# The expert layer as two dense products over whole tables instead of gathered rows

## What is computed

```python
def _peer(h, w_q, keys1, keys2, u_tab, v_tab):        # per block of tb = 128 tokens
    qh = (hb @ w_q).reshape(tb, 8, 2, 128)
    s1 = jnp.einsum('thd,nd->thn', qh[:, :, 0], keys1)
    s2 = jnp.einsum('thd,nd->thn', qh[:, :, 1], keys2)
    v1, i1 = lax.top_k(s1, 16)
    v2, i2 = lax.top_k(s2, 16)
    cand = (v1[..., :, None] + v2[..., None, :]).reshape(tb, 8, 256)
    cidx = (i1[..., :, None] * 128 + i2[..., None, :]).reshape(tb, 8, 256)
    best, pos = lax.top_k(cand, 16)
    eidx = jnp.take_along_axis(cidx, pos, axis=-1)
    gates = jax.nn.softmax(best.astype(jnp.float32), axis=-1).astype(hb.dtype)
    act = jax.nn.gelu(jnp.einsum('td,thkd->thk', hb, u_tab[eidx]), approximate=False)
    return jnp.einsum('thk,thkd->td', gates * act, v_tab[eidx])
```

## Time and profile before

| | |
|---|---|
| median of 3 runs | 3188.63 us (3188.34 to 3195.54) |
| span of the profiled execution | 3191.6 us |
| mean granted TensorE clock in it | 0.987 of full speed |
| last query product before the experts ends | 2524.2 us |
| last product with v rows ends | 3180.8 us |
| PE busy in the span | 3008.7 us (94%) |
| DVE, ACT, POOL busy | 1624.6, 814.9, 349.4 us |
| moved by DMA | 584.86 MB |

### The profile page before, as it was taken

How to read it: one execution, slowest core, us unless ns; L and a number is a source line. 1 busy time by engine, 2 the same in 40 slices (tenths; PEclk the granted TensorE clock), 3 DMA queues, 4 the chain that set the end, 5 groups by cost and what they waited for, 6 DMA issues and landing times. The chain is left out here.

```text
span 3191.6 us, 33886 instructions
## 1 busy us (share of the span) xinstructions
PE 3008.7 (94%) x12694; PEld 2114.5 (66%) x12694; DVE 1624.6 (51%) x3601; ACT 814.9 (26%) x1889; POOL 349.4 (11%) x391
## 2 busy tenths in 40 slices
PE   7999999999999999998999999999989999888776
PEld 3666556758888888485876678888877744443222
DVE  3233444367773676413234457543036577677774
ACT  2222244311002100012113430010023354444443
POOL 0000000010000000100000000000000244344442
PEclk9999999999999999999999999999998999999999
DMA  6212111153441544642322134577432799999997
GB/s 240 86 60 66 53 53 53 53 165 119 132 135 57 161 154 131 204 142 89 104 79 80 60 109 158 186 285 277 143 113 95 271 420 420 383 421 420 420 420 311
DMA packets 280769, 584.86 MB, mean 183 GB/s; under 512 B 11736, under 2 KB 231768, under 8 KB 244256
## 3 DMA queue, kind: packets, MB, share of 16 engines
q0 software_dynamic: 51504, 338.98, 27.0%
q1 hardware_dynamic: 229104, 243.73, 23.7%
HBM read 581.58 MB, written 1.08 MB: 183 GB/s over the span
## 5 line engine op out<-in xcount | busy, mean ns | idle before, releaser
L815 PE MATMUL banks<-normed,weight_ring 128*128 128x512 f32 (+1 forms) x1280 | 483.9, 533 | 14.4 <-PEq L322 13.9
L815 PEld LDWEIGHTS banks<-normed,weight_ring 128*128 128x128 f32 x1280 | 242.5, 191 | 233.9 <-issue 223.0
L824 PE MATMUL banks<-weight_ring,normed 128*128 128x256 f32 x1408 | 320.5, 383 | 0.0
L3581 PE MATMUL banks<-weight_ring,work 128*128 128x512 f32 x512 | 248.9, 610 | 56.8 <-ACT work L3450 55.8
L824 PEld LDWEIGHTS banks<-weight_ring,normed 128*128 128x128 f32 x1408 | 265.0, 191 | 54.0 <-issue 19.4
L3581 PE MATMUL banks<-work 128*128 128x512 f32 x512 | 253.3, 617 | 49.9 <-ACT work L3450 48.8
L436 DVE CUSTOM_DVE_ANT_0 work<-work 128x1024 f32<-128x1024 f32 x176 | 209.5, 1224 | 111.4 <-DMA work<-ada_turned 92.6
L2155 PE MATMUL banks<-normed,weight_ring 128*128 128x256 f32 x1088 | 241.0, 385 | 9.9 <-ACT normed L2325 3.8
L2155 PEld LDWEIGHTS banks<-normed,weight_ring 128*128 128x128 f32 x1088 | 209.9, 193 | 40.5 <-issue 6.6
L1660 PE MATMUL banks<-branches,weight_ring 128*128 128x256 f32 (+1 forms) x656 | 210.3, 483 | 3.4 <-PEq L322 3.4
L3581 PEld LDWEIGHTS banks<-weight_ring,work 128*128 128x128 f32 x512 | 87.7, 189 | 167.5 <-ACT work L3450 104.8
(11 more groups left out here) (515 smaller groups left out, 3947.4 us busy)
## 6 DMA issues: line engine op xcount, KB each, us to landing
weight_ring<-w_in SPq DMA_DIRECT2D x98, 1024.0 KB, 5.2
weight_ring<-w_ffn_in SPq DMA_DIRECT2D x44, 1024.0 KB, 5.4
work<-ada_turned POOLq DMA_DIRECT2D x80, 512.0 KB, 3.8
work<-ada_turned POOLq DMA_DIRECT2D x16, 1536.0 KB, 9.6
weight_ring<-w_ffn_out SPq DMA_DIRECT2D x20, 1024.0 KB, 5.2
weight_ring<-w_out SPq DMA_DIRECT2D x12, 1024.0 KB, 5.3
weight_ring<-w_br_ml SPq DMA_DIRECT2D x8, 1024.0 KB, 5.3
weight_ring<-w_br_da SPq DMA_DIRECT2D x8, 1024.0 KB, 5.2
```

What stands on the lines that cost most here:

```text
L815: last = pe.matmul(proj_bank(tile)[:, since:T], w[:, kk, half * P:(half + 1) * P], c.h[:, kk, since:T], start=kk == 0, stop=kk == KT - 1)
L824: last = pe.matmul(proj_bank(tile)[:, x * CHUNK:(x + 1) * CHUNK], c.h[:, kk, j * P:(j + 1) * P], w[:, kk, :], start=kk == 0, stop=kk == KT ...
L3581: last = pe.matmul(c.banks[2 * t + half][:], diag[:, r, :], vrows[r][:, half * 512:(half + 1) * 512], start=e == t * H * K, stop=e == (t + ...
```

## The change

The expert layer no longer fetches the rows of chosen experts. It streams both tables once, whole, through `weight_ring`, in 64 pieces of 1 MB each (`expert_u`, `expert_v`; a piece is called a pair, since it holds 2 x 128 experts). The host lays the tables out for that.

- Products with u: for every pair, `pair_product` computes all 256 experts of the pair for all 256 tokens (16 products of 128x256), and ScalarE's `lift` takes the gelu into `dense`, a sheet of 128 x (128 x 256) fp32 that holds one number for every expert and token. All arrays that it overlays are now parts of one tensor `room`.
- Gates: a token's gates form a 128 x 128 sheet (first index by second index). It is made as a product of two matrices over the token's 128 chosen places: `right`, one-hot in the second index (POOL), and `left`, one-hot in the first index times the gate (VectorE). This is `choose`, one product of 128x128 for each token, 4 tokens to a group. VectorE multiplies `dense` with the group's sheets (`apply_group`), and ScalarE and VectorE place and apply them for the pairs whose gelu comes later (`place_group`, `apply_pair`). The 64 groups are spread over pairs 36 to 63: two groups behind a pair, and three behind 8 of the 28 pairs.
- Products with v: `value_product`, for each of 64 pairs, 2 rows of experts, 2 token tiles and 2 halves one product of 128x512, 512 in all. The last two pairs are ordered by token tile.
- All 16 queries and scores are done before the products with u. The searches run two units at a time, and the numbers of the experts are worked out for 8 heads at once (`name`). POOL issues no DMA in this layer any more.

Core of the diff:

```diff
-        for e in range(2 * H * K):
-            if e % K == 0:
-                pool.wait_ge(c.ranked, e // K + 1)
-            if e >= R:
-                pool.wait_ge(c.expert_done, e - R + 1)
...
-            pool.indirect_dma_start(
-                out=fetched[e % R], out_offset=None, in_=a["experts"],
-                in_offset=bass.IndirectOffsetOnAxis(ap=experts_u[:, e:e + 1], axis=0)
-            ).then_inc(c.gathered[e % R], 16)
+        for group in range(GROUPS):
...
+            if group >= 2:
+                pool.wait_ge(c.chosen, group - 1)
+            for i in range(PEER_GROUP):
+                token = PEER_GROUP * group + i
+                last = pool.tensor_scalar(right[token % (2 * PEER_GROUP)], c.constant("iota"), turned[:, 1, token:token + 1], None,
+                                          ALU.is_equal)
+            last.then_inc(c.right_made, 1)
...
+        def make_left(group):
...
+            if group >= 2:
+                dve.wait_ge(c.chosen, group - 1)
+            for i in range(PEER_GROUP):
+                token = PEER_GROUP * group + i
+                last = dve.tensor_scalar(left[token % (2 * PEER_GROUP)], c.constant("iota"), turned[:, 0, token:token + 1],
+                                         turned[:, 2, token:token + 1], ALU.is_equal, ALU.mult)
+            last.then_inc(c.left_made, 1)
+
+        def apply_group(group):
...
+            dve.wait_ge(c.chosen, group + 1)
+            dve.wait_ge(c.lifted, pairs)
+            part = dense[:, 0:2 * pairs, group_tokens(group)]
...
+        for pair in range(PEER_FIRST, PAIRS):
+            for group in groups_at(pair):
+                if group + 1 < GROUPS:
+                    make_left(group + 1)
+                apply_group(group)
+            apply_pair(pair)
...
+        def pair_product(pair):
+
+            w = weights(16 + pair)
+            if pair >= 2:
+                pe.wait_ge(c.lifted, pair - 1)
+            for i in range(2):
+                for k in range(KT):
+                    last = pe.matmul(c.banks[pair % 2][:, i * NLAT:(i + 1) * NLAT], w[:, k, i * P:(i + 1) * P], hs[:, k, :],
+                                     start=k == 0, stop=k == KT - 1)
+            last.then_inc(c.pair_product, 1)
...
+        def choose(group):
...
+            pe.wait_ge(c.left_made, group + 1)
+            pe.wait_ge(c.right_made, group + 1)
+            if group >= 4:
+                pe.wait_ge(c.chosen_applied, group - 3)
+                pe.wait_ge(c.chosen_placed, group - 3)
+            for i in range(PEER_GROUP):
+                r = (PEER_GROUP * group + i) % (2 * PEER_GROUP)
+                last = pe.matmul(out[:, :, i], right[r], left[r], start=True, stop=True)
+            last.then_inc(c.chosen, 1)
+
+        def value_product(pair, i, t):
+
+            w = weights(16 + PAIRS + pair).rearrange("p k n -> p (k n)")
+            for half in range(2):
+                at = i * D + half * 512
+                last = pe.matmul(c.banks[2 * t + half][:], dense[:, 2 * pair + i, tokens_of(t)], w[:, at:at + 512],
+                                 start=pair == 0 and i == 0, stop=pair == PAIRS - 1 and i == 1)
+            return last
...
+        for n in range(2 * PAIRS):
+            if n >= SLOTS:
+                if n - SLOTS < PAIRS:
+                    sp.wait_ge(c.pair_product, n - SLOTS + 1)
+                else:
+                    sp.wait_ge(c.pair_valued, n - SLOTS - PAIRS + 1)
+            its = c.ring[:, n % SLOTS]
+            if n < PAIRS:
+                sp.dma_start(its, a["expert_u"][n]).then_inc(c.loaded[n % SLOTS], 16)
```

More of the change, by code:

```diff
@@ new lines, in ending @@
+        def ending(t):
+            done = Chain(dve, c.finished)
+            done.n = 6 * t
+            dve.wait_ge(c.expert_done, t + 1)
+            dve.wait_ge(c.row_copied, 8)
+            for half in range(2):
+                part = slice(half * 512, (half + 1) * 512)
+                done.mark(dve.tensor_tensor(acc[:, part], c.banks[2 * t + half][:], gate_row[:, part], ALU.mult))
+            done.wait()
+            done(dve.tensor_tensor(xt[:, t, :], xt[:, t, :], acc, ALU.add))
+            dve.wait_ge(c.finish_rooted, 2 * t + 1)
+            done(dve.tensor_scalar(mean, mean, 1.0 / D, EPS, ALU.mult, ALU.add))
+            done(dve.reciprocal(inverse, mean))
+            dve.wait_ge(c.finish_rooted, 2 * t + 2)
+            done(dve.scalar_tensor_tensor(tokens[:, t, :], xt[:, t, :], mean, gain_row, ALU.mult, ALU.mult))
@@ L3365, in vector @@
         inverted(0)
-        for k in range(KT):
-            out_scale(0, k)
-        search = Search(dve, 0)
-        for _ in search.halves():
-            pass
-        assert search.n == IN_HALVES
-        for _ in chain(search.numbers(), search.weights(1)):
-            pass
-        dve.wait_ge(c.token_copied, 2)
-        for u, t in units:
-            body(u, t)
-        for part in ending(1).values():
-            part()
+        out_scale(0)
+        search([0])
+        for tile in range(KT):
+            added(1, tile)
+        inverted(1)
+        out_scale(1)
+        for first in (1, 3, 5):
+            search([first, first + 1])
+        search([7])
+        name(0)
+        search([8, 9])
+        weigh(0)
+        for first in (10, 12, 14):
+            search([first, first + 1])
+        name(1)
+        weigh(1)
+        make_left(0)
+        for pair in range(PEER_FIRST, PAIRS):
[4 more added lines that the diff above has]
+            apply_pair(pair)
+        for t in range(2):
+            ending(t)
     def scalar(act):
         def copy_query(n):
-            head, first, end = PEER_QUERIES[n]
-            part = slice(first * P, end * P)
+            head, t = QUERIES[n]
             act.wait_ge(c.queried, n + 1)
@@ L3519, in score @@
                 pe.wait_ge(c.score_copied, n - 1)
[L3520 to L3523 removed]
+            for i in range(2):
+                last = pe.matmul(score_bank(n)[:, t, i * P:(i + 1) * P], qh[:, n % 2, i, tokens_of(t)], keys[:, i, :],
+                                 start=True, stop=True)
@@ L3563, in tensor @@
         query(0)
-        turn_tokens(0)
+        out_tile(1, 2, 0, 8)
         score(0)
-        for tile in range(2, KT):
+        for tile in range(3, KT):
             out_tile(1, tile, 0, 8)
@@ new lines, in tensor @@
+        query(3)
+        for tile in range(KT):
+            out_sum(1, tile)
+        score(2)
+        for n in range(4, len(QUERIES)):
+            query(n)
+            score(n - 1)
+        for pair in range(PAIRS):
+            pair_product(pair)
+            if pair == 0:
+                score(len(QUERIES) - 1)
+            if pair in PEER_TURNS:
+                turn_lists(PEER_TURNS.index(pair))
+            for group in groups_at(pair):
+                choose(group)
+        pe.wait_ge(c.chosen_applied, GROUPS)
```

579 lines of the change are left out of this document (273 added, 306 removed).

## The result

The changed kernel takes 3550.8 us in the median (3550.09 to 3558.97), the kernel before, on the same chip, 3190.9. The ratio is 1.113, with a 95% interval of 1.111 to 1.115: 360 us slower, where 3552 us was forecast.

A forecast was written before the change was run, and what follows sets the result against it. Transfers were taken to bound the expert loop (656 us), TensorE close behind at 549.6 busy. Along TensorE's queue, 2523.3 + 55.1 + 446.5 + 58.7 + 15 + 3 + 439.3 + 3.6 + 10.8 = 3555.3, forecast 3552 us, range 3525 to 3640.

The forecast's parts named there:

- 5 between pairs and values: Between the last pair and the first value product: a chain of three short instructions, 3 us.
- Step 2: Products with u on TensorE: 2048 instructions of 128x256 at 0.218 us, 446.5 us, 6.98 us a pair.
- Step 4: In pairs with three groups TensorE stalls for the third group's matrices, 8 times: 10 to 18 us, taken as 15.
- step 6: Products with v on TensorE: 1024 instructions at 0.429 us, 439.3 us, plus 3.6 us for eight turns of rows.
- 3.0 off: Taken from the summed span of 3555.3 us because the runs' median lies 3.0 us under the profiled span: 3552 us.
- my own range: Range of the main case (chance 0.80): 3532 us without stalls and at 0.217, to 3580 with dearer instructions and port rule.
- The port rule: VectorE's two-port instructions and GpSimd's exclude each other, so step 4's stalls would cost 9 us more: 3561 us.
- A cover: VectorE's searches, costed at nothing: ending near 2655 us, ahead of their uses in the pairs by 40 to 100 us.
- A (POOL): POOL bounds pairs 36 to 63 if a one-hot matrix costs 0.91 us or more; 3624 us at 1.25; chance 0.08.
- B (choosing doesn't stream): Each of 512 choosing instructions takes its 0.275 us latency, not 0.112: 83 us more, 3635 us; chance 0.08.
- C (bytes decide): Transfers stay the expert stage's limit and bytes halve, so the kernel gets faster: 2905 us; chance 0.01.
- D: Loads or lists come late so that TensorE isn't the path, adding some tens of us; chance 0.03.

The follow-up runs named there:

- the high halves: Changed kernel, products with u and v reading only the high 16 bits of each fp32 as bf16, one instruction instead of two: 2999.6 us, 0.940 of before.
- the half rows: Kernel before, gathers fetching only the u half of each row, all instructions as before: 3090.2 us, 0.968 of before.

## Why the prediction was right

The forecast of the time and its reason hold: the layer went from a bound by transfers to a bound by TensorE, and the sum along TensorE's queue came out. Its terms, with the working in the prediction, against the changed kernel's rows:

| step | forecast, us | measured, us |
|---|---|---|
| third query ends at | 2523.3 | 2528.8 |
| 1 rest of queries and scores | 55.1 | 54.9 |
| 2 products with u | 446.5 | 442.0 |
| 3 choosing gates, turning lists | 58.7 | 57.8 |
| 4 the eight waits | 15 | 14.9 |
| 5 between pairs and values | 3 | 2.1 |
| 6 products with v, turns of rows | 442.9 | 446.0 |
| 7 the end | 10.8 | 10.1 |
| span | 3555.3 | 3557.2 |

Step 2 is the 960 instructions from 2590.69 to 2797.89, 0.2158 us each, times 2048. The measured rows add up to 3556.6; 0.6 us are left between the steps. Step 4 is eight times the gap from the end of the second group (2866.07 + 16 x 0.1116 = 2867.86) to 2869.72. Step 6 runs from 3101.11 to the last product's end at 3547.1.

**What hit by offset.** The two programs are the same up to the layer, and the changed one got there 5.5 us later in its profile. That is no effect of the change that any run here shows: of the seven variants with the same program up to there, five got there 3 to 6 us earlier than the kernel before, and two 4 us later. The steps themselves were 3.6 us too dear in sum, and the profiled execution lay 6.4 us above the median's time, where I had taken 3.0 off. Plus 5.5, less 3.6, less 3.4: the median's agreement within 1.2 us is partly luck. So is the steps' sum. Step 2 was 4.5 us too dear (0.218 us an instruction, where it took 0.2158) and step 6 was 3.1 us too cheap. And the lower end of my own range, 3532, doesn't follow from its terms: without the stalls (15 us) and at 0.217 us an instruction (2 us) the sum gives 3535.

**Step 6 lacked a term: the clock.** In the first products with v the granted clock was at its lower level:

```profile
3101.00:3107.00 6.00, 5.89 (x8) 2.54 (x9) 0.01 (x1) 0.00 (x0) 0.00 (x0) 0.52 0.00 0
3107.00:3113.00 6.00, 6.00 (x16) 2.65 (x15) 0.00 (x0) 0.00 (x0) 0.00 (x0) 1.00 0.13 29
...
3101.11 23.63 PE L3576 MATMUL banks<-weight_ring,room 128*128 128x512 f32 x48 [1.88 <-issue]
```

TensorE works off half as many instructions in the first 6 us as in the next, and this is the 2.8 us of the first 48: at 0.429 us they would take 20.8. Before the clock fell TensorE had stood still twice within 5 us, the last of the eight waits (1.65 us) and the step from gates to values (1.88). Where the first of these is gone (pairs with two groups only) or 0.93 us long (without POOL's matrices), the same 48 take 20.84 us. In the two variants that keep both (half of the bytes, no VectorE matrices) they take 22.34 and 22.44. So, by these profiles (one of each kernel), the last of the eight waits cost more than its own length.

**Step 4** was right for a half-right reason. The wait is where I put it, and its size too. I had VectorE and POOL both as candidates and POOL between 0.2 and 0.7 us an instruction; it is 0.59 in a row, nearer to my upper end, and POOL alone sets the wait.

**The port rule** was worth 9 us in its own sentence and nothing in the runs.

**A cover was mis-sized.** I let VectorE's searches end near 2655. They ended 30 us later, at 2685:

```profile
2591.35 0.23 DVE L3291 TENSOR_SCALAR normed<-room 128x128 uint32<-128x128 uint32 x1 [19.61 <-ACT room L3395]
...
2641.56 0.29 DVE L3307 TENSOR_REDUCE room<-room 128x8 f32<-128x128 f32 x1 [26.22 <-ACT room L3419]
...
2682.74 2.29 DVE L3301 TENSOR_REDUCE room<-stream 128x128 f32<-128x2048 f32 x1
```

VectorE stands still twice. For 19.6 us it waits in the middle of naming the first token tile's experts, because `name(0)` waits there for the scores of all 16 units. For 26.2 us it waits in `weigh(0)`, which sums the exponentials of the first tile, and these ScalarE makes only when it comes to pair 8. I had read pair 8 as the time by which VectorE must be ready, and overlooked that VectorE's program stops there until ScalarE gets to it. The second wait sets the end: without the first one VectorE would only have come to `weigh(0)` sooner and waited longer. The second half was due at pair 25, at 2583 + 25 x 6.9 = 2756 us, so both cost nothing. With the high halves, where pair 8 comes at about 2600 us and pair 25 at 2643.5, the cover is nearly gone: VectorE has the second tile's sums ready for the exponentials at 2637.7, 6 us ahead, and TensorE waits for no list.

**The rivals.** A (POOL) fell at its condition: 0.60 us an instruction, where it decides from 0.91 on; in the version with cheap products it held. B (choosing doesn't stream) fell: 16 instructions in 1.95 us, 0.112 each, though every fourth column is written. C (bytes decide) fell for this change by the price of TensorE's instructions, as argued, and the high halves show the other side: with those prices cut, the same stream of tables gives 3000 us. The sentence of the Trainium skill (SBUF — State Buffer, "A bandwidth-pool intuition that's wrong"), "HBM is almost always your end-to-end bottleneck", sets HBM against SBUF there and not against TensorE. Read as widely as in rival C, it fits the kernel before (nearly half of TensorE's busy time there gained nothing) and not the one after (half of the tables' bytes gained nothing). D had no place: no wait for a load or a list stands before TensorE's products in the changed kernel.

## What to carry to other kernels

When a stage is bound by one resource, read how far behind it the second one runs before its work is traded: here the gathers held 656 us and TensorE 550 of them, so halving the bytes could give at most the 100 us that the half rows gave, while the dense form asked TensorE for about 1020. Write the sum along the queue that becomes the bound, with spacings from unbroken rows and not with mean latencies. And when a product gets cheap, ask at once which engine or load is next: loads, POOL and loads again, in three stretches.

## What the hardware showed

- Writing every fourth fp32 column of a bank costs TensorE nothing that the trace shows: 0.112 us an instruction of 128x128, as in rows that write in sequence.
- POOL's tensor_scalar on 128 columns takes 0.60 us, more than twice VectorE's 0.28 to 0.31.
- With half of the instructions of the products with v rows, TensorE was busy 44 of 100 us in the expert loop of before, and the granted clock there fell from 1.00 to 0.52, near the lower level of 1.2 GHz. The time didn't change, since TensorE wasn't on the path. In the changed kernel with high halves it was busy 126 of 160 us in the products with v and the clock stayed at 1.00.
- In the changed kernel TensorE stood still for 1.65 and 1.88 us within 5 us, and the granted clock in the next 6 us was 0.52. 128x512 products took twice as long in most of them, 2.8 us in all; where the first of the two was gone or 0.93 us long, the clock stayed at 1.00.
- The same program reached the layer at times that spread over 12 us between profiles of the changed kernel and its variants, and over 17 us in those of the kernel before; the granted clock ahead of it was 0.98 in the early ones and 0.95 to 0.96 in the late ones.
